# Two layers as a loop with a barrier, or written out as one program with each phase's first work placed in the phase ahead

## The reference, cut to what matters

```python
# first block, twice
h    = rms_norm(x, norm_mix)
proj = h @ w_in                    # about 10,000 columns: four mixers and their gates
y    = nsa(..), stick_breaking(..), gla(..), forgetting(..)
x    = x + sum_n(gates_n * (y_n @ w_branch_n)) @ w_out
x    = x + square(relu(rms_norm(x, norm_ff) @ w_ff1)) @ w_ff2
# second block: x is normed with norm_final, ctx is a second stream of 256 tokens
mod  = silu(c) @ w_ada + b_ada     # shifts, scales and gates
h    = x * (1 + sc) + sh           # the same for ctx, then grouped attention and MLP,
                                   # then latent attention and MLP, each with a layer_norm
```

## Time and profile before

| | |
|---|---|
| three runs | 2438.57 us median (2436.44 to 2440.42) |
| profiled execution | 2438.9 us, span 2437.1 us |
| PE busy in the span | 2251.5 us, 92% |
| DVE, ACT, POOL busy | 1231.9, 688.8, 475.3 us |
| DMA | 341 MB, mean 140 GB/s |

### The profile page before, as it was taken

The page is one execution under the profiler, slowest core; times in us unless marked ns, Lnnn a source line. Parts: engine busy times, 40 slices in busy tenths (PEclk is TensorE's granted clock), DMA queues, the critical chain, the costliest instruction groups (busy, mean ns, idle before and its releaser), DMA issues. The chain is left out here.

```text
span 2437.1 us, 33628 instructions
## 1 busy us (share of the span) xinstructions
PE 2251.5 (92%) x13927; PEld 1821.8 (75%) x13927; DVE 1231.9 (51%) x1634; ACT 688.8 (28%) x1496; POOL 475.3 (20%) x259
## 2 busy tenths in 40 slices
PE   5999999999959999999999698798999998997998
PEld 5898788889858987788898544446888885554987
DVE  4575435765335764347643215573433433365565
ACT  2223444132011234440320156713012012262111
POOL 1221112243212221112433000011111110101332
PEclk9999999999979999999999798998999999998999
DMA  7533665565255336555653411012222221202451
GB/s 208 205 139 123 233 221 175 179 231 201 108 161 196 132 126 237 214 189 173 242 181 130 186 69 40 1 51 71 104 104 72 102 80 58 102 35 87 173 193 67
DMA packets 209911, 341.23 MB, mean 140 GB/s; under 512 B 46435, under 2 KB 77598, under 8 KB 209630
## 3 DMA queue, kind: packets, MB, share of 16 engines
q1 hardware_dynamic: 207068, 334.68, 39.1%
q0 software_dynamic: 944, 3.47, 0.5%
q10 hardware_dynamic: 1746, 0.89, 0.1%
HBM read 335.88 MB, written 3.15 MB: 139 GB/s over the span
## 5 line engine op out<-in xcount | busy, mean ns | idle before, releaser
L259 PE MATMUL bank<-hT_high,ring_low 128*128 128x256 f32 (+1 forms) x2032 | 609.7, 300 | 0.0
L259 PEld LDWEIGHTS bank<-hT_high,ring_low 128*128 128x128 f32 x2032 | 393.3, 194 | 12.4 <-issue 0.5
L239 POOL CAST ring_high<-ring 128x2048 fp32r<-128x2048 f32 (+2 forms) x108 | 203.5, 1886 | 756.1 <-PE bank L260 653.1
L258 PE MATMUL bank<-hT_low,ring_high 128*128 128x256 f32 (+1 forms) x1008 | 298.0, 296 | 18.4 <-DVE ring_low L246 12.6
L246 DVE TENSOR_TENSOR ring_low<-ring,ring_high 128x2048 fp32r<-128x2048 f32 (+2 forms) x108 | 239.7, 2222 | 129.7 <-POOL ring_high L239 129.4
L260 PE MATMUL bank<-hT_high,ring_high 128*128 128x256 f32 (+1 forms) x1008 | 289.9, 288 | 0.0
L258 PE MATMUL bank<-ring_low,hidden_high 128*128 128x512 f32 x640 | 254.3, 397 | 0.0
L239 POOL CAST half_high<-ring 128x2048 fp32r<-128x2048 f32 x64 | 125.6, 1965 | 614.1 <-PE bank L260 408.5
L1028 ACT ACTIVATE work<-bank 128x512 f32<-128x512 f32 (+6 forms) x270 | 121.6, 474 | 394.6 <-PE bank L260 339.0
L258 PEld LDWEIGHTS bank<-hT_low,ring_high 128*128 128x128 f32 (+1 forms) x1008 | 195.1, 194 | 29.3 <-issue 23.6
L246 DVE TENSOR_TENSOR ring_low<-ring,half_high 128x2048 fp32r<-128x2048 f32 x64 | 152.8, 2392 | 98.9 <-POOL half_high L239 98.5
(11 more groups left out here) (228 smaller groups left out, 4486.2 us busy)
## 6 DMA issues: line engine op xcount, KB each, us to landing
ring<-w_ff SPq DMA_DIRECT2D x32, 2048.0 KB, 8.3
ring<-mlp_w SPq DMA_DIRECT2D x32, 2048.0 KB, 8.2
ring<-w_in SPq DMA_DIRECT2D x30, 2048.0 KB, 7.8
ring<-w_ada SPq DMA_DIRECT2D x24, 2048.0 KB, 7.6
ring<-w_branch SPq DMA_DIRECT2D x24, 512.0 KB, 5.9
ring<-w_in SPq DMA_DIRECT2D x32, 256.0 KB, 4.3
ring<-w_out SPq DMA_DIRECT2D x4, 2048.0 KB, 7.6
ring<-gqa_w_qkv SPq DMA_DIRECT2D x3, 2048.0 KB, 16.5
```

Of the source, the lines that this page charges most:

```text
L239: nc.gpsimd.tensor_copy(self.high(i), self.part(i, False)).then_inc(self.high_made, 1)
L258: nc.tensor.matmul(out, a[0], b[1], start=start, stop=False)
L259: nc.tensor.matmul(out, a[1], b[0], start=False, stop=False)
```

## The change: one block, written out, with stages interleaved

`prologue`, `first_layer` (now called twice, with `l` a plain number) and `second_block` no longer open blocks. Each returns a `Programs` tuple of five generators, and `build` opens a single block in which each engine runs these generators in the fixed order of `stages` (0 is the prologue, 1 and 2 the layers, 3 the second block). A `yield` ends a stage.

```diff
-        prologue(nc, T, dram, sem, chip)
-        with nc.Fori(0, DEPTH) as l:
-            first_layer(nc, l, T, dram, out, layer_sem, chip)
-            for s in layer_sems:
-                nc.gpsimd.sem_clear(s)
-            nc.all_engine_barrier()
-        second_block(nc, T, dram, out, sem, chip)
+        first = prologue(nc, T, dram, sem, chip)
+        layers = [first]
+        for l in range(DEPTH):
+            layers.append(first_layer(nc, l, T, dram, out, sem, chip, layers[-1]))
+        phases = layers + [second_block(nc, T, dram, out, sem, chip, layers[-1])]
+        stages = [0, 1, 1, 0, 1, 2, 1, 2, 2, 3, 2, 3]
+        def run(programs):
+            for n in stages:
+                next(programs[n], None)
```

Bank pairs (`Pair`) and the two self-semaphores now live as long as the kernel. `Weights` gets `prev.held`, the last user of each slot in the phase ahead, and waits for that. A layer's programs, where they differ:

```diff
 sync:
+        if l > 0:
+            prev.idle(sp)                  # last up product of the layer ahead
+            load_rows(row_load)
+        W.load(sp, 0, 2)                   # q0, q1
+        yield
-            sp.dma_start(x_kept, x).then_inc(x_saved, 16)
-            W.load(sp, 0, 3)
+        if l > 0:
+            for t in range(TT):
+                prev.x_done(sp, t)
+                sp.dma_start(x_kept[:, t, :], x[:, t, :]).then_inc(x_saved, 16)
+        W.load(sp, 2, 3)                   # cmp
+        yield
             sp.wait_ge(*done("xT3"))
             sp.dma_start(wk1_sb, wk1).then_inc(wk1_in, 16)
+        sp.dma_start(wk2, ...)             # and wv2, w_alpha, fox_b: were on ScalarE
 scalar:
+        if l == 0:
+            load_rows(row_load)
+            prev.idle(act)                 # the f32 tables
+        link(f(rstd, eps.to_broadcast([P, TT]), ACT.Sqrt))
+        yield
-            row_scale(lambda t: None)
+        row_scale(lambda t: prev.x_done(act, t), entry_sq, False)
 gpsimd:
+        if l > 0:
+            pool.wait_ge(*prev.held[N_SLOTS - 1])
+        for i in range(2):
+            Y.round_high(nc, pool, i)
+        yield
 vector:
+        if l > 0:
+            Y.make_low(nc, dve, 0, 1)
+        yield
-            norm(1)
+        norm(1, entry_xn)
             low_bits("xT", ROW_MIX, hT_high[0])
+        if l == 0:
             Y.make_low(nc, dve, 0, 1)
+        yield
 ...
             X.make_low(nc, dve, *range(FFK // 2 + 4, FFK))
+        yield
             for t in range(TT):            # the four adds of down into x
```

The second block:

```diff
+        prev.idle(sp)
             sp.dma_start(xc, dram["ctx_2"]...).then_inc(ctx_in, 16)
+        sp.dma_start(nf_row, dram["norm_final"]...)      # was on ScalarE
+        W.load(sp, 0, 3)
+        yield
+        prev.x_done(sp, TT - 1)
             sp.dma_start(grid, dram["grid_gqa"]).then_inc(first_in, 16)
 ...
-    XT_ORDER = [(0, 1, 2, 3), (0, 1, 2, 3)]
+    XT_ORDER = [(2, 3, 0, 1), (0, 1, 2, 3)]
```

More of the change, by code:

```diff
@@ L1 @@
+from collections import namedtuple
 from contextlib import ExitStack
@@ L178, in __init__ @@
         self.loaded = [sem(f"{label}_loaded{s}") for s in range(N_SLOTS)]
-        count, self.ready, held, self.last = [0] * N_SLOTS, [], {}, []
-        for i, (_, _, _, sources, _) in enumerate(tiles):
+        count, self.ready, self.held, self.last = [0] * N_SLOTS, [], dict(held), []
+        for i, (_, _, _, sources, used) in enumerate(tiles):
             count[slots[i]] += 16 * len(sources)
             self.ready.append(count[slots[i]])
-            self.last.append(held.get(slots[i]))
-            held[slots[i]] = i
+            self.last.append(self.held.pop(slots[i], None))
+            self.held[slots[i]] = used
     def slot(self, i):
@@ L339, in first_layer @@
     early = Carver(gates.rearrange("p a b -> p (a b)"))
-    rows, wk2, wv2 = early.take(P), early.take(2, HD), early.take(2, HD)
+    wk2, wv2 = early.take(2, HD), early.take(2, HD)
+    rows = chip["rows"]
     glq, glk = early.take(2, S), early.take(2, S)
@@ L348, in first_layer @@
     sq = flat_y[:, TT * D:TT * D + D]
+    entry = Carver(chip["work"], after_hT - KD * S)
+    entry_sq = entry.take(KD, S).rearrange("p k s -> p (k s)")[:, 0:D]
+    entry_xn = entry.take(TT, D)
     pcT = [yT[:, 4:8, :], yT[:, 12:16, :]]
@@ L492, in first_layer @@
     tiles += [(f"up{i}", KD, 512, [(whole, w_ff1[:, :, 512 * i:512 * i + 512])], done(f"up{2 * i + 1}")) for i in range(8)]
-    tiles += [(f"down{i}", 4, D, [(whole, w_ff2[:, 4 * i:4 * i + 4, :])], (down_used, 2 * i + 2)) for i in range(8)]
+    tiles += [(f"down{i}", 4, D, [(whole, w_ff2[:, 4 * i:4 * i + 4, :])], (down_used, 2 * i + 2) if i < 7 else (OT.full, OT.order["down3"] + 1)) for i in range(8)]
     first_step = [tile[0] for tile in tiles].index("gate0")
-    slots = [n % 3 for n in range(first_step)]
+    turn_of = [n for n in prev.held if n < 3] if l > 0 else [0, 1, 2]
+    slots = [turn_of[n % 3] for n in range(first_step)]
     slots += [n % 2 if kind == "gate" else 2 for kind, n in step_tiles]
@@ new lines, in gpsimd @@
+    def gpsimd(pool):
+        if l > 0:
+            pool.wait_ge(*prev.held[N_SLOTS - 1])
+        for i in range(2):
+            Y.round_high(nc, pool, i)
+        yield
+        yield
+        for i in range(2, len(parts)):
+            Y.round_high(nc, pool, i)
+        pool.wait_ge(*done(f"br{BRANCHES[-1]}_{KD // 2 - 1}"))
+        for i in range(2):
+            X.round_high(nc, pool, i)
+        pool.wait_ge(*done("wo11"))
+        for i in range(2, len(halves)):
+            X.round_high(nc, pool, i)
+        yield
@@ L1576, in prologue, with x_done, mod_done, idle @@
+    def x_done(eng, t):
+        (SC, OT)[t].taken(eng, f"down{2 * t}", f"down{2 * t + 1}")
+    def mod_done(eng):
+        PROJ.taken(eng, f"adT{ada_late[-1]}")
+    def idle(eng):
+        eng.wait_ge(*done(f"up{FFK // 2 - 1}"))
+    return Programs(sync, tensor, scalar, vector, gpsimd, x_done, W.held, mod_done, idle)
 def prologue(nc, T, dram, sem, chip):
     x, consts, masks, cos, sin = (chip[n] for n in ("x", "consts", "masks", "cos", "sin"))
-    work = Carver(chip["work"])
-    pos, rows = work.take(S), work.take(P)
+    work = Carver(chip["work"], 26952)
@@ L1581, in prologue @@
+    rows = chip["rows2"]
+    pos = work.take(S)
     cols, silu_c = chip["cols2"], chip["silu_c"]
@@ new lines, in scalar, with gpsimd @@
+    def scalar(act):
+        yield
+        ps = OT.arrived(act, "rows2")
+        nc.scalar.activation(cols, ps[:, 0:N_ROWS2], ACT.Copy)
+        nc.scalar.activation(silu_t, ps[:, ROW_C:N_ROWS2].rearrange("p (s k) -> p s k", s=2), ACT.Exp, scale=-1.0)\
+            .then_inc(OT.free("rows2"), 1)
+        act.wait_ge(sin_arg, 1)
+        nc.scalar.activation(sin, part, ACT.Sin)
+        act.wait_ge(cos_arg, 1)
+        nc.scalar.activation(cos, angle, ACT.Sin)
+    def gpsimd(pool):
+        yield
```

3089 lines of the change are left out of this document (1553 added, 1536 removed).

## The result

| | before | after |
|---|---|---|
| median of the runs on one chip | 2437.51 us (4 runs) | 2400.87 us (4 runs) |
| profiled execution | 2438.9 us, span 2437.1 | 2401.09 us, span 2399.3 |
| ratio, 95% interval | | 0.9845 (0.9831 to 0.9858) |

Its terms add up to the difference of the spans.

What follows compares the result with a forecast made beforehand. TensorE was busy 92% of the span, leaving only three stops between phases to win. Gains of 5.2, 15.3 and 12.8 us sum to 33.3, taking 2438.9 to 2405.6 us, range 2397 to 2416.

Steps and rivals of the forecast that it cites:

- Stop 1: Kernel entry to first GEMM: `q0` starts at 28.0 instead of 33.22, held by row loads behind weights; 5.2 us shorter.
- the rival in which small loads overtake the weights: Kernel entry: the nine small loads land before the weights, gaining 9.9 us instead of 5.2, total 2400.9 us; chance 0.12.
- the chain without rows: Kernel entry: compute chain alone, with transposes at about 13.9, would let the first GEMM start at 23.3.
- Stop 2: Layer 0's last product to layer 1's first GEMM: 15.3 us shorter than the 28.7 before.
- The gain without loss: Between the layers: 14.6 us from an earlier second Square plus 3.1 from `make_low(0, 1)` done ahead, 17.7 us.
- the loss by `make_low(1)` ahead of the adds: Between the layers: waiting for `q1`, loaded in 7.2 us, starts the adds at 680.9 instead of 678.50; 2.4 us lost.
- my lower bound: Between the layers: `q1` loads in 5.7 us if an empty queue saves half the latency; loss 0.9, gain 16.8 us.
- Stop 3: Layer 1's last product to the second block: `0v1` starts at 1366.15 instead of 1378.93, 12.8 us shorter.
- the wait I kept 1 us for: Between the layers: store of `x` must land before ScalarE overwrites it; counted 0, with 1 us kept for the range.
- stays up in stop 3: Before the second block: the clock stays at full between transposes, total 2401.6 us; rival, chance 0.13.
- One long program makes TensorE wait for its own instructions: Whole kernel: written-out code costs 3.4 us, 2409; for a slower kernel, at about 2445 us, rival chance 0.03.
- Nothing changes: At the stops: something else holds the first GEMMs, so the stops stay and the change does nothing; rival, chance 0.01.

Runs made afterwards that it cites:

- experiment 1: Changed kernel with SyncE's positions and nine row loads issued ahead of the 16 weight DMAs instead of behind them: 2396.14 us, ratio 0.9822 to the kernel before.
- experiment 2: Changed kernel with layer 1's first two low parts made behind the adds that end layer 0, not ahead: 2401.53 us, ratio 0.9849 to the kernel before.
- experiment 5: Changed kernel with each phase in its own block, no loop, clearing or barrier, low parts late, store of `x` before rows and weights: 2427.93 us, ratio 0.9956.
- (10): Kernel before with its two layer passes written out instead of looped, each still followed by semaphore clearing and all-engine barrier: 2428.35 us, ratio 0.9971.
- (12): Four separate blocks without loop or clearing, with only the all-engine barrier put back behind each of the first three: 2427.04 us, ratio 0.9958 to the kernel before.
- (7): Changed kernel with low parts late and layer 1's row and weight loads after layer 0's adds, store of `x` issued first: 2405.70 us, ratio 0.9869.
- Experiment 4: Changed kernel with the second block's first token tiles and value GEMMs in the old order: 2404.65 us, ratio 0.9859 to the kernel before.
- Experiment 3: Changed kernel with low parts late and layer 1's rows and first weights loaded after layer 0's adds, ahead of the store of `x`: 2415.74 us, ratio 0.9903.

## Why the prediction was right, point by point

**The form of the argument held.** The gain is the three stops, 35.8 of the 37.8 us. The forecast had 33.3.

**Stop 1 (5.2 forecast, 5.8 measured).** The rows were late by their place behind the weights: `q0` at 27.44, forecast 28.0, with the transpose of 119 rows directly ahead of it and ended by a DMA, and experiment 1 shows that it was their place in SP's order that mattered. How they were late was not as worked out. The sum let the rows wait until the weights had landed, at 25.7, and gave 0.4 us to the issuing of `positions` and the rows. The last weights did land at 25.9. But SP was busy issuing until 25.9 as well: 19.9 us for the 16 weight DMAs and 3.9 for the ten small ones, the last row at 25.68. TensorE had it 1.55 us later. So no row could be in by 24, and the rival in which small loads overtake the weights didn't come true, but this kernel doesn't test the order of completion either. That 28.0 was so near is in part luck. In the chain without rows I was too cautious at its start: the transposes began at 11.8 and not at 13.9, because `x` was in by 8.4 and not by 10.3. I had 23.3 for it, and it was 21.6.

**Stop 2 (15.3 forecast, 17.1 measured).** The gain without loss, 17.7, was about right: 28.7 − 17.7 = 11.0, and 11.7 was measured. The term that was mis-sized is the loss by `make_low(1)` ahead of the adds. I took 7.2 us for the load of `q1` and 2.4 us of delay. The load took 5.8 (issue at 660.18, landed at 666.0), close to my lower bound of 5.7, and the delay of the adds was 0.9, which was the bound's own number. The bound was added up wrongly by 0.1: 4.2 and half of 3.3 are 5.85. I had chosen the value near the full latency by the median of all 32 such loads. That median is taken over loads with a busy queue, and `q1` met an empty one. The low parts made ahead gained 3.1 by forecast; experiment 2 puts the net of gain and loss at 1.75, and forecast numbers would give 3.1 − 0.9 = 2.2.

**What the 28.7 us consisted of.** The prediction read 5.9 us from the last add to SP's first load and named block end, clearing, barrier and jump together. It took them as gone, so the sum didn't depend on which it was, but experiment 5's expectation gave them to the blocks, and that was wrong. Step by step, stop 2 goes from 28.7 to 22.0 without the loop (10), to 16.6 without the clearing (12), to 16.0 without the barrier (5), to 14.7 in one block (7), to 13.4 with rows and first weights ahead (2), and to 11.7 with the low parts ahead. Of the second step 4.6 us are the clearing by the gap itself. The other 0.7 isn't put to one thing, since 12 also has the changed kernel's places of store and loads and 10 those of the kernel before. Of the loop's 6.7 us 0.6 lie ahead of SP's first load and 5.4 between it and ScalarE's first computation: 2.5 of late start behind the jump, 1.6 of slower issuing and 1.3 of table load. The last 0.7 is `make_low(0)`, which takes 3.3 us to the first GEMM while GpSimd casts the second half beside it, and 2.5 in experiment 10, where that cast comes later.

**Stop 3 (12.8 forecast, 12.9 measured).** The chain of four tiles ran as laid out: Sqrt at 1331.17, ScalarE's first tile at 1331.37, held once by the scaling. Experiment 4 puts the order of tiles at 2.3 of it. The gap with clearing is 5.2 us here, in the loop and written out alike.

**Nothing new was waited for.** The store of `x` was the wait I kept 1 us for, and the changed kernel shows none: it landed at 675.95, 1.25 us ahead of the first high part. Experiment 3 shows what hangs on it: with the store behind eight weight DMAs it costs 11.4 us. The first gate tile of layer 1 was cast at 863.76 after 5.68 us of waiting for its DMA, 2.0 us more than the 3.72 of the kernel before, and cost nothing, as forecast.

**The clock.** The rival "stays up in stop 3" fell: it dropped at about 1332.5, 2.5 us into a pause that ended at 1333.0. The Trainium skill ("TensorE: Matmul & The Clock Gate", on HAM oscillation) makes pauses between bursts the thing that drops the clock, and the prediction put this case on the side of staying up by it. The trace does not agree: no pause of the stop is longer than 2.98 us, and the clock fell.

What the prediction left out is that moving the stops also moves and shortens the time at half clock. Added up over windows of 1 us it is 165.5 us before and 131.3 after: in stop 2 with the GEMM behind it from 30.7 to 13.7, in stop 3 from 27.3 to 13.6. Those 31 us lie almost all inside the stops, where TensorE has little to do.

The sums leave out the kernel's entry. There the profile has no clock record yet and prints 1.00, but the pace of the products is that of half speed, as these windows of the kernel before show:

```profile
33.30:39.00 5.70, 5.70 (x27) 5.70 (x28) 3.32 (x3) 0.00 (x0) 1.41 (x1) 1.00 1.13 253
39.30:45.00 5.70, 5.70 (x51) 5.70 (x50) 1.02 (x1) 0.60 (x1) 1.90 (x1) 1.00 1.04 322
```

27 products in 5.7 us are what layer 1's first GEMM does at 0.50. The first record of the clock is at 39.2 before and 32.0 after. With that start counted, layer 0 had 29.9 us at half before and 21.7 after, and layer 1 22.9 and 24.8. Their lengths went the same way, by −3.4 and +2.3 us. Over the twelve kernels of the table a layer's length is fitted by 635 us plus 0.42 for each us at half (correlation 0.93 for layer 0, 0.76 for layer 1). By that fit, an estimate, the clock makes all of the −3.4 and 0.8 of the +2.3. So the statement that layers keep 644 to 648 us was just met (643.9 and 646.2), but by wandering, not by keeping still.

**The rest of the rivals.** "One long program makes TensorE wait for its own instructions" fell: layer 1 written out takes 646.2 and layer 0 643.9, within what the looped kernel had. Its premise, that layer 1 was 3.4 us shorter in the loop, is mostly the clock as well (29.9 and 22.9 us at half, 2.9 us by the fit). "Nothing changes" fell. The time alone would not have told: 2400.87 is as good as the 2400.9 and 2401.6 of the two faster rivals, and neither happened. It came from 2.5 us more at the stops and 2.0 between them.

## What to carry to other kernels

Price a loop around a phase by the whole stretch from its last result to the next pass's first computation, and look at the clearing of semaphores first: here 63 of them on one engine cost 4.6 us each time, and the slow start behind the loop 6.7, while the way through a block's end or a barrier cost 0.3. What the end of a block costs more is what it keeps back: four blocks took 22 us longer than one with interleaved stages, and 14 us of it arose at the stop where three weight tiles and then the small loads could only be issued behind the block's end. Once barriers are gone, engines run ahead without a hand-made order, and what is left to place by hand are small loads that something waits for: put them ahead of large ones on the same queue, since the engine that issues them is itself held up by the large ones. When a store moves with the loads, check what waits for it, and take the latency of a load from loads in the same state of the queue.

## What the runs showed that I had not expected

- An engine's way out of one block into the next took 0.35 us, and with an all-engine barrier 0.67. GpSimd's clearing of 63 semaphores took 4.6.
- In the second pass of a loop the same DMA issues were slower than in the written-out kernel: ScalarE's four took 3.5 us instead of 1.9, and SP's seven row loads 3.7 (687.19 to 690.8) instead of 2.4 (679.78 to 682.2). The loop's first pass lies between, with 2.0 and 3.1, so registers in the addresses can make at most 0.1 us of the 1.6 on ScalarE and about half of the 1.3 on SP. Why ScalarE stands still for 2.8 us behind its branch, and SP for 0.3, the runs don't show.
- A small load is as late as what stands ahead of it, and part of that is the issuing: 16 DMAs of 256 KB took SP 19.9 us to issue at the kernel's entry, and four into an empty queue 2.8 (660.18). The 320 KB of `grid_gqa` took 12.3 us to land before and 3.3 in the changed kernel, where nothing large is under way.
- With the same instructions a layer took from 641.2 to 649.4 us over these kernels, and the time at half clock inside it moved with it, which runs from 16.6 to 29.9 us. Of the 4.5 us of unforecast gain 2.0 come from outside the stops, and a single comparison can't tell such an effect of 2 or 3 us from an edit's.
- The last eight down halves of a layer, 24 matmuls each, all took the same time within a layer, 5.49, 5.55 or 5.60 us, but not the same in each layer and kernel, though their instructions are the same: 5.55 and 5.49 in the kernel before, 5.60 twice in the changed one. This stays open.
